# The reads of gates and gelu values in the second expert product are begun by ScalarE instead of SyncE

## What is computed

```python
def peer_ffn(x, w_q, sub_keys, u_table, v_table):
    # y = sum_h sum_{e in top16_h} softmax(score)_e * gelu(u_e . x) * v_e
    ...
    def chunk(args):
        xc, ic, gc = args
        u = u_table[ic]
        a = jax.nn.gelu(jnp.einsum('cd,ced->ce', xc, u), approximate=False) * gc
        return jnp.einsum('ce,ced->cd', a, v_table[ic])
```

## Time and profile before

| what | value |
|---|---|
| time, median of 3 runs | 1678.22 us |
| the runs | 1677.5, 1678.22, 1678.37 us |
| profiled execution, span from first to last instruction | 1676.1 us |
| TensorE busy | 1666.8 us, 99% of the span |
| second expert product | about 1147 to 1671 us |

### The profile page before, as it was taken

One profiled execution on the slowest core, in us unless ns is written; L12 is line 12 of the kernel. 1 busy time (PEld: TensorE's weight loads), 2 busy tenths in 40 slices (PEclk: granted clock), 3 DMA queues, 4 the chain that ended last, 5 costly groups with the idle time before them and its releaser, 6 DMA issues.

```text
span 1676.1 us, 24608 instructions
## 1 busy us (share of the span) xinstructions
PE 1666.8 (99%) x9035; PEld 1471.2 (88%) x9035; DVE 1233.3 (74%) x2295; ACT 779.5 (47%) x1380; POOL 773.4 (46%) x484
## 2 busy tenths in 40 slices
PE   9999999999999999999999999999999999999998
PEld 7788777788889999999999999998888888888887
DVE  7877636744524799999999476734888888888886
ACT  5533326544212343457777767733433333333334
POOL 4544322444334778865555577775222222232220
PEclk9999999999999999999999999999999999999999
DMA  8322432374335889988778599997999999999993
GB/s 225 101 76 66 112 91 61 95 244 139 113 120 158 281 291 339 333 279 283 289 257 307 208 391 388 393 357 253 371 375 346 372 350 369 355 358 364 356 358 124
DMA packets 258671, 433.68 MB, mean 259 GB/s; under 512 B 14768, under 2 KB 181936, under 8 KB 256888
## 3 DMA queue, kind: packets, MB, share of 16 engines
q1 hardware_dynamic: 202536, 249.11, 45.6%
q0 software_dynamic: 36864, 134.23, 21.0%
q10 hardware_dynamic: 19152, 48.77, 7.9%
HBM read 372.82 MB, written 59.24 MB: 258 GB/s over the span
## 4 chain that ended last, share of the span: by engine, by line
PE 68%; ACT 0%; issue 0%; DVE 0%; ACTq 0%
PE bank L252 21%; PE bank L254 21%; PE bank L253 21%; PE bank L1818 5%; PE bank L1784 0%; ACT L1471 0%; ACT hot L1522 0%; ACT hot L1491 0%; PE bank L1825 0%; PE x_rows L1784 0%; DVE rows L1775 0%; ACT mixbuf L1479 0%; ACT gl L1471 0%; ACTq L1484 0%; ACT fin L1526 0%
## 5 line engine op out<-in xcount | busy, mean ns | idle before, releaser
L247 POOL TENSOR_TENSOR spl_a<-raw,spl_a 128x1024 fp32r<-128x1024 f32 x170 | 409.4, 2411 | 322.0 <-ACT spl_a L243 321.1
L243 ACT ACTIVATE spl_a<-raw 128x1024 fp32r<-128x1024 f32 x294 | 310.9, 1059 | 388.1 <-PE bank L254 375.5
L252 PE MATMUL bank<-act,spl_a 128*128 128x384 f32 (+1 forms) x1216 | 425.4, 350 | 0.8 <-DVE act L602 0.4
L254 PE MATMUL bank<-act,spl_a 128*128 128x384 f32 (+1 forms) x1216 | 417.3, 343 | 0.0
L253 PE MATMUL bank<-act,spl_a 128*128 128x384 f32 (+1 forms) x1216 | 417.1, 343 | 0.0
L252 PE MATMUL bank<-spl_a,aws 128*128 128x512 f32 x768 | 299.0, 389 | 0.0
L254 PE MATMUL bank<-spl_a,aws 128*128 128x512 f32 x768 | 298.8, 389 | 0.0
L253 PE MATMUL bank<-spl_a,aws 128*128 128x512 f32 x768 | 298.8, 389 | 0.0
L1302 POOL DMA_INDIRECT rows<-in_v_tab,expert x128 | 135.7, 1060 | 343.1 <-DVE hot L1710 334.6
L252 PEld LDWEIGHTS bank<-act,spl_a 128*128 128x128 f32 x1216 | 228.5, 188 | 12.2 <-issue 3.3
L253 PEld LDWEIGHTS bank<-act,spl_a 128*128 128x128 f32 x1216 | 228.6, 188 | 7.6 <-issue 0.7
(11 more groups left out here) (325 smaller groups left out, 2376.7 us busy)
## 6 DMA issues: line engine op xcount, KB each, us to landing
raw<-in_u_t SPq DMA_DIRECT2D x128, 512.0 KB, 5.1
raw<-in_v_tab SPq DMA_DIRECT2D x128, 512.0 KB, 7.5
dense_gates<-mixbuf ACTq DMA_DIRECT2D x12, 2048.0 KB, 8.2
mixbuf<-dense_gates SPq DMA_DIRECT2D x32, 768.0 KB, 9.3
gelu_ux<-gl ACTq DMA_DIRECT2D x120, 192.0 KB, 5.4
mixbuf<-gelu_ux SPq DMA_DIRECT2D x30, 768.0 KB, 12.5
raw<-in_w_in SPq DMA_DIRECT2D x42, 512.0 KB, 3.8
raw<-in_w_q SPq DMA_DIRECT2D x16, 512.0 KB, 4.0
```

The source lines that it names most:

```text
L243: eng.activation(spl(n, 0, slice(0, W)), raw[:, s, :], ACT.Copy).then_inc(hi_done, 1)
L247: eng.tensor_tensor(spl(n, 1, slice(0, W)), raw[:, n % RAW, :], spl(n, 0, slice(0, W)).bitcast(F32), ALU.subtract).then_inc(lo_done, 1)
L252: nc.tensor.matmul(out, w_hi, x_hi, start=first, stop=False)
L254: return nc.tensor.matmul(out, w_lo, x_hi, start=False, stop=last)
```

## The change

In steps j = 2, 6, 10, ... of the second expert product, ScalarE begins the two reads, between `weight_hi(j + 2)` and `split_hi` of unit j + 4. SyncE's program has only the loads left there. The numbers of the parts, the sizes, the buffers, the semaphores and what is waited for by name are as before. The two reads of gates in the first expert product stay on SyncE.

```diff
-        def mix_gates(sp, part_no):
+        def mix_gates(queue, part_no):
...
-        def mix_gelu(sp, part_no):
+        def mix_gelu(queue, part_no):
...
             for s in range(4):
-                sp.wait_ge(gelu_stored[s], 16 * (c // 4 + 1))
-            sp.dma_start(gelu_in[:, half, :, :], gelu_d[c:c + 4, :, :].rearrange("c p t -> p c t")) \
+                queue.wait_ge(gelu_stored[s], 16 * (c // 4 + 1))
+            queue.dma_start(gelu_in[:, half, :, :], gelu_d[c:c + 4, :, :].rearrange("c p t -> p c t")) \
                 .then_inc(mix_in[half], 16)
...
                         sp.dma_start(lists[:, :], norm_final).then_inc(final_in, 16)
-                    part_no = (j - NC) // 4 + 2
-                    if j >= NC and j % 4 == 2 and part_no < NC // 4:
-                        sp.wait_ge(a_mult, 4 * (part_no - 2) + 4)
-                        mix_gates(sp, part_no)
-                        mix_gelu(sp, part_no)
...
                 for j in range(NC):
                     if j + 2 < NC:
                         weight_hi(j + 2)
+                    part_no = j // 4 + 2
+                    if j % 4 == 2 and part_no < NC // 4:
+                        act_e.wait_ge(a_mult, 4 * (part_no - 2) + 4)
+                        mix_gates(act_e, part_no)
+                        mix_gelu(act_e, part_no)
                     if V0 + LEAD + j < N_UNITS:
                         split_hi(act_e, V0 + LEAD + j)
```

More of the change, by code:

```diff
@@ L1277, in build @@
         z_gelu, a_ready = sem("z_gelu"), sem("a_ready")
-        def mix_gates(sp, part_no):
+        def mix_gates(queue, part_no):
             half, c = part_no % 2, expert_chunk(4 * part_no)
-            sp.dma_start(gates_in[:, half, :, :, :].rearrange("p b c t -> p b (c t)"),
+            queue.dma_start(gates_in[:, half, :, :, :].rearrange("p b c t -> p b (c t)"),
                          dense_d[:, :, c * TB:(c + 4) * TB].rearrange("b p x -> p b x")) \
                 .then_inc(mix_in[half], 16)
-        def mix_gelu(sp, part_no):
+        def mix_gelu(queue, part_no):
             half, c = part_no % 2, expert_chunk(4 * part_no)
             for s in range(4):
-                sp.wait_ge(gelu_stored[s], 16 * (c // 4 + 1))
-            sp.dma_start(gelu_in[:, half, :, :], gelu_d[c:c + 4, :, :].rearrange("c p t -> p c t")) \
+                queue.wait_ge(gelu_stored[s], 16 * (c // 4 + 1))
+            queue.dma_start(gelu_in[:, half, :, :], gelu_d[c:c + 4, :, :].rearrange("c p t -> p c t")) \
                 .then_inc(mix_in[half], 16)
```

## The result

The changed kernel takes 1692.28 us at the median of 4 runs (1687.35 to 1706.77), the kernel before 1677.86 us on the same chip. The ratio is 1.0101, with a 95% interval of 1.0079 to 1.0122: **slower by 1.0%, 14.4 us**. Run again, in another comparison, it took 1695.79 us (1688.24 to 1706.03) against 1677.47, ratio 1.0116 (1.0060 to 1.0171). The kernel before never spread by more than 3 us; this one spreads by 19. The profiled execution is the slowest of the first four (1706.77 us, span 1704.9), so its rows show the mechanism at its strongest and 28.8 us where the median has 14.4.

The account below looks back on a forecast made before the run. TensorE, busy 99% of the span, was taken as the bound. 30 x 1.07 us, 32 us, less 3.7 us of its lead gave 28 us: 1704 on a 1676.1 us span, plus 2.1 us, 1706 us; range 1677 to 1728.

Parts of the forecast that it names:

- SyncE's relief: On SyncE: 0.43 us and about 1.4 us of beginning transfers saved per part; no one waits for SyncE, worth nothing.
- ScalarE's block: ScalarE blocked about 2.0 us beginning the reads, `spl_a` 1.3 us late, covered by 3.7 us: 0 to 3 us in all.
- The read becomes the link of a closed chain: On ScalarE each read stands behind a `weight` that waits for the previous read; the pair may take at most 15.2 us.
- The ring: The cycle read, landing, `weight`, `aws<-scb`, next read, with one read in it; forecast period 17.39 us against TensorE's 16.32.
- the 1.11 us from `weight` to the next begin: Fixed term of the period: start of `weight` to end of `aws<-scb`, 1.11 us, after which the next read begins.
- The read changes its queue and is served in what the others leave: In q10 the reads compete packet by packet with loads and gathers; later-begun loads now pass before them.
- The signs: Expected in the trace: reads begun every 17.4 us, VectorE waiting for `mixbuf`, gelu landings 15 to 17 us, loads 4 to 6.
- The sum, 28 us: Second expert product: 30 parts at 1.07 us, 32 us, less 3.7 us of TensorE's lead; likeliest case, chance 0.60.
- 30 x 1.07 us: At parts 2 to 31, a dear-price period of 17.39 us exceeds TensorE's 16.32 by 1.07 us each: 32 us.
- a danger above the range: If TensorE's pauses lowered the granted clock, the time would leave the range upward; no row showed such a fall.
- The pair in time: Rival: both reads land within 15.2 us and TensorE never waits; 1678 us, up to 1681; chance 0.27.
- Blocks on ScalarE as the cost: Rival: every begin takes 4.7 us, lag grows 1.7 us per part, some 45 us, 1723; 0.10 shared with reads served last.

Follow-up runs that it names:

- e3: Kernel before, reads on SyncE, with one further ScalarE copy of about 1.9 us between `aws<-scb` and `spl_a` every fourth step: 1677.37 us.
- e7: Changed kernel with the reads begun one step earlier (j = 1, 5, 9, ...), still behind `aws<-scb`: 1686.79 us.
- e2: Kernel before, SyncE still begins the reads but also waits for `a_hi` of weight j + 2, so no earlier than ScalarE would: 1677.50 us.
- e9: Kernel before with queues swapped in the second product: loads begun by ScalarE, reads alone on SyncE, both at the moment of before: 1698.96 us.
- e6: e1 with the reads also waiting for `lo_done` of unit j + 3, so ScalarE begins them when SyncE did before: 1692.45 us.
- e11: Changed kernel with each load in the second product made as two transfers of half the columns, packets of 2 KB instead of 4 KB: 1693.85 us.
- e5: Changed kernel again, word for word: 1695.79 us.
- e1: Changed kernel with ScalarE beginning the two reads in the same step ahead of `aws<-scb` instead of behind it: 1680.99 us.
- e12: Changed kernel with the gelu read of each part cut to the first of its four units: 1679.55 us.
- e10: e1 with the loads also moved to ScalarE, ahead of the reads, so both are in one queue in SyncE's old order: 1691.62 us.
- e4: Changed kernel with the reads moved behind `spl_a` of that step: 1691.66 us.

## Why the prediction was right, and where it was not

The time was forecast as 1706 us and slower; it is 1692.3, slower. By the prediction's own steps:

- **TensorE is full, so only a new wait can move the time; SyncE's relief is worth nothing.** Right. Loads land 1.6 us sooner and no one is faster for it.
- **ScalarE's block, 0 at the median.** Right for the usual block: 0.37 + 0.17 + 0.84 us, and e3 shows 1.9 us to be free. Rare long ones were put at 0 to 3 us, and that held too: in the two profiled executions of the changed kernel they reached 4.0 and 4.9 us and cost TensorE 1.45 of 18.6 us and 0.8 of 12.6 us of waiting. For other places the price would have been too low (9 us in e7).
- **The read becomes the link of a closed chain.** The step that failed as a cause. The ring is there, but e2 has it and loses nothing, while e9 loses 21 us without it, and in e6 late reads reach TensorE without it. Whether the ring adds something to the loss of the changed kernel is not shown. A detail of it was wrong too: the 1.11 us from `weight` to the next begin are 0.6 us, because the begin starts with `aws<-scb` (1270.14 and 1270.15 above).
- **The read changes its queue and is served in what the others leave.** Right, and the main cause: e9 has this alone and loses 21 us, e2 lacks this alone and loses nothing. The signs came out near: gelu values land after 14.5 us at the median (forecast 15 to 17), loads after 6.4 (forecast 4 to 6). How finely the queues take turns stays open: 21 against 40 packets is one to two and not one to one, and halving the loads' packets (e11) gained nothing.
- **The sum, 28 us.** The size was off: 14.4 us at the median, half. The term was 30 x 1.07 us, the same at each part, never given back. Measured, it is not the same at each part. In the profiled execution the times between the begins of reads ran from 14.0 to 23.4 us; their mean was (1662.32 - 1161.18) / 29 = 17.3 us, as forecast (17.39), in the slowest of four runs; in e5 the mean is 16.9 us. But turns of 14.0 to 15.9 us follow the long ones, since VectorE's wait empties the queues, and they do give back. TensorE's waits were 18.6 us in all, not some 28. The runs differ by 19 us, where the forecast had one period for all. That 28 us meets the 28.8 us of the profiled execution, and 17.39 the 17.3, is luck: there 18.6 us are waits, some of them not of reads, and 10.4 us are longer busy time, which the sum did not have.
- **Part of the loss is clock, which was no term of the sum.** The granted clock was put aside as a danger above the range. It fell, and the time stayed inside the range: most of TensorE's 10.4 us of longer busy time are matmuls at the lower level (last section).
- **The rivals.** The pair in time: VectorE's 13 waits exclude it for the changed kernel; it is nearly what e1 and e12 are. Blocks on ScalarE as the cost: not the changed kernel's main one, but real in e6, e7 and e10. The rule cited for it, from the Trainium skill, page "DMA: Bandwidth & Descriptors", section "Issuing engines are not separate DMA queues", that several beginning engines save only the time of beginning, says nothing of the loss that e9 shows: the same bytes, 21 us more.

## What to carry to other kernels

When the transfer engines are nearly full (here 101% of packet time beside a full TensorE; emptier ones were not tried), the queue in which a transfer stands can decide who is late, even if its issue costs nothing: keep a transfer with many small packets and a deadline in the same queue as the big ones that are begun after it, so that it stays ahead of them. Price such a move by the longest landings and by the room that each has before its deadline, not by medians. Before reads are put on an engine that computes, look at the longest begin of such a read in the trace, and at what stands behind it.

## What the runs showed of the hardware

**A stall of TensorE can cost more than its length.** After 5.07 us of idle time the granted clock, 1.00 before, is 0.50 in the row from 1272 to 1275 us above, that is 1.2 instead of 2.4 GHz. Matmuls start 0.43 us apart instead of 0.23 (1272.48 and 1272.91), seven of them, so about 1.4 us more. It does not follow every stall. Three stretches behind one, the first two from the changed kernel (after 2.15 and 1.45 us of idle time), the third from e5 (after 3.17 us):

```profile
1199.70:1202.70 3.00, 3.00 (x8) 2.38 (x9) 2.40 (x3) 1.24 (x3) 0.67 (x1) 0.55 1.01 304
...
1433.00:1436.00 3.00, 3.00 (x13) 2.51 (x14) 3.00 (x4) 1.48 (x2) 0.74 (x2) 1.00 1.06 385
```

```profile
1606.00:1609.00 3.00, 3.00 (x13) 2.51 (x14) 2.41 (x3) 1.24 (x3) 0.66 (x1) 1.00 1.05 305
```

In the profiled execution of the changed kernel the clock fell behind five of the seven waits, those of 2.15 to 5.07 us, and not behind those of 1.45 and 1.78 us; in e5 it fell behind 3.36 and 5.28 us and not behind 3.17. So the length of the stall does not decide it alone. Five stretches of about 1.4 us make some 7 of the 10.4 us of longer busy time, a quarter of the 28.8 us of that execution (an estimate from these rows); the rest was not told apart.

**ScalarE begins a transfer before the instruction written ahead of it has ended.** 1270.14 and 1270.15 in the changed kernel, and 1308.92 and 1308.95 in e1: both orders were written as one behind the other, and the instruction takes 0.52 and 1.06 us. Where that instruction has to queue behind another one, the transfer can even come first: in e4 it was begun at 1347.46, the `spl_a` ahead of it started at 1347.79.

**Beginning one read can take from 0.4 to 7 us.** For the same transfer the shortest was 0.37 us in e4, the longest 4.0 and 4.9 us in the two executions of the changed kernel, 5.7 in e7, 5.8 in e1, 6.0 in e6, 6.3 in e10, and on SyncE 4.7 before, 4.9 in e3 and 7.3 in e9. What it waits for, no run here shows. It is no measure of the landing: the read that landed last of all in the changed kernel, after 22.2 us, was begun in 0.54 us.
